# Stick-breaking attention: from running sums by TensorE on transposed scores to VectorE's scan over reversed keys

## The reference, cut to what matters

```python
def stick_breaking_attention(q, k, v):
    ...
        z = jnp.einsum('bqhd,bshd->bhqs', qb, k, preferred_element_type=jnp.float32) * scale
        mask = kpos[None, :] < tpos[:, None]
        log_keep = jnp.where(mask, jax.nn.log_sigmoid(-z), 0.0)
        after = lax.cumsum(log_keep, axis=3, reverse=True) - log_keep
        a = jnp.where(mask, jnp.exp(jax.nn.log_sigmoid(z) + after), 0.0)
        return jnp.einsum('bhqs,bshd->bqhd', a.astype(v.dtype), v)
```

## Time and profile before

| what | value |
|---|---|
| median of 3 runs | 3250.41 us (3246.34 to 3252.65) |
| profiled execution | 3254.31 us, span 3252.7 us |
| PE / PEld / DVE / ACT / POOL busy | 94% / 81% / 69% / 40% / 25% of the span |
| first pair's units of `stick` start on PE | 206.76 us |
| loop of `stick`, first scores to the first matmul of `out_proj` | 225.47 to 365.30 us |

### The profile page before, as it was taken

How to read it: one execution, slowest core, us unless ns; L and a number is a source line. 1 busy time by engine, 2 the same in 40 slices (tenths; PEclk the granted TensorE clock), 3 DMA queues, 4 the chain that set the end, 5 groups by cost and what they waited for, 6 DMA issues and landing times. The chain is left out here.

```text
span 3252.7 us, 43626 instructions
## 1 busy us (share of the span) xinstructions
PE 3064.3 (94%) x16416; PEld 2637.4 (81%) x16416; DVE 2232.9 (69%) x4289; ACT 1292.6 (40%) x2261; POOL 824.2 (25%) x732
## 2 busy tenths in 40 slices
PE   7999899999999999988889988889999999999998
PEld 6666688887666888867768767889999999999998
DVE  4765477674555776753433358988788888888886
ACT  3655432233444322333432232349843443333333
POOL 1001200001001200042000023779734333433431
PEclk9999899999999999989999989999999999999999
DMA  4011144433211544311122222546699999999993
GB/s 145 25 35 46 46 156 136 141 110 119 78 61 63 169 136 141 110 66 54 36 68 91 86 82 75 185 138 229 231 359 325 321 315 316 326 319 328 316 320 117
DMA packets 187616, 522.29 MB, mean 161 GB/s; under 512 B 15616, under 2 KB 78080, under 8 KB 185104
## 3 DMA queue, kind: packets, MB, share of 16 engines
q1 hardware_dynamic: 129344, 307.27, 27.8%
q0 software_dynamic: 45104, 164.68, 14.8%
q10 hardware_dynamic: 12960, 47.55, 3.8%
HBM read 482.71 MB, written 36.73 MB: 160 GB/s over the span
## 5 line engine op out<-in xcount | busy, mean ns | idle before, releaser
L238 PE MATMUL bank<-h_hi,w_hi 128*128 128x512 f32 (+1 forms) x2528 | 964.2, 381 | 61.7 <-DVE h_lo L304 13.0
L238 PE MATMUL bank<-h_lo,w_hi 128*128 128x512 f32 (+1 forms) x2528 | 949.1, 375 | 0.0
L212 DVE TENSOR_TENSOR w_lo<-w_raw,w_hi 128x1024 fp32r<-128x1024 f32 (+1 forms) x460 | 590.2, 1283 | 309.5 <-ACT w_hi L206 307.2
L206 ACT ACTIVATE w_hi<-w_raw 128x1024 fp32r<-128x1024 f32 (+1 forms) x508 | 545.0, 1073 | 522.9 <-PE bank L238 505.0
L238 PE MATMUL bank<-h_hi,w_lo 128*128 128x512 f32 (+1 forms) x2528 | 597.0, 373 | 9.5 <-POOL w_lo L219 9.5
L238 PEld LDWEIGHTS bank<-h_hi,w_hi 128*128 128x128 f32 x2528 | 484.5, 192 | 145.9 <-issue 44.1
L238 PEld LDWEIGHTS bank<-h_lo,w_hi 128*128 128x128 f32 x2528 | 485.3, 192 | 64.7 <-issue 8.7
L238 PEld LDWEIGHTS bank<-h_hi,w_lo 128*128 128x128 f32 x2528 | 460.3, 189 | 79.7 <-issue 13.0
L238 PE MATMUL bank<-e_hi,w_hi 128*128 128x384 f32 x1024 | 345.7, 338 | 8.9 <-DVE e_lo L2357 8.9
L238 PE MATMUL bank<-e_lo,w_hi 128*128 128x384 f32 x1024 | 344.7, 337 | 0.0
L2266 POOL DMA_INDIRECT own_row<-in_u_rows,own_e x128 | 157.6, 1231 | 297.0 <-DVE sums L2394 249.0
(11 more groups left out here) (420 smaller groups left out, 4333.4 us busy)
## 6 DMA issues: line engine op xcount, KB each, us to landing
w_raw<-in_w SPq DMA_DIRECT2D x476, 512.0 KB, 3.8
ada_w<-in_ada_w POOLq DMA_DIRECT2D x48, 512.0 KB, 3.6
expert_weights<-G ACTq DMA_DIRECT2D x12, 2048.0 KB, 7.1
Gin<-expert_weights SPq DMA_DIRECT2D x32, 768.0 KB, 9.7
w_raw<-in_w SPq DMA_DIRECT2D x32, 704.0 KB, 4.1
hidden_ahead<-u_stage ACTq DMA_DIRECT2D x48, 192.0 KB, 2.8
ahead<-hidden_ahead SPq DMA_DIRECT2D x24, 384.0 KB, 6.5
fx_crow<-fox_cum POOLq DMA_DIRECT2D x8, 512.0 KB, 5.5
```

Source lines behind the costliest of these rows:

```text
L206: sc.activation(w_hi[s][:, 0:n], w_raw[raw_slot[u]][:, 0:n], ACT.Copy).then_inc(*w_hi_made.next(u))
L212: ve.tensor_tensor(w_lo[s][:, 0:n], w_raw[raw_slot[u]][:, 0:n], w_hi[s][:, 0:n], ALU.subtract).then_inc(*w_lo_made.next(u))
L238: m = te.matmul(out, wt, moving, start=(not low and k == 0 and moving is hi), stop=(low and k == len(blocks) - 1))
```

## The change

Queries are put on partitions and keys along the free axis, as in `fox`. k and v are written reversed along the sequence (`flip`), so that a running sum from the left is the sum over later keys. Step i of a pair takes the block of queries i by its (i+1)*128 visible keys, the nearest first. DVE scales the scores and adds the mask into `z`, makes `low` = min(-z, 0), and runs one `tensor_tensor_scan` that adds `low` and subtracts `soft` = log(1 + exp(-|z|)) along the keys; adding `z` gives the exponent. ACT makes `soft` in three operations and the exp. PE turns the probabilities block by block, ACT moves them, PE multiplies them with v. The scan, the addition and the exp of a step are issued one step behind its scores, turning, moving and value sums two steps behind. The matmuls of mask and running sums, the high and low parts and GpSimd's share go.

```diff
             split_lo(U[n] + 1)
             yield
             ve.wait_ge(*w_used.at(U[n]))
+            to = dst[:, ::-1] if flip and n else dst[:, :]
-                scaled(dst[:, :], lin[U[n] % 2][:, :]).then_inc(*dve.next(name, "qkv"[n], p))
+                scaled(to, lin[U[n] % 2][:, :]).then_inc(*dve.next(name, "qkv"[n], p))
...
+        neg = sb(st, "sb_neg", [P, T])
+        z = [[sb(st, f"sb_z{hh}{b}", [P, T]) for b in range(2)] for hh in range(2)]
+        neg_in = loaded("sb_neg_in")
+        soft = [[sb(st, f"sb_soft{hh}{b}", [P, T]) for b in range(2)] for hh in range(2)]
+        low = [[sb(st, f"sb_low{hh}{b}", [P, T]) for b in range(2)] for hh in range(2)]
+        Pm = [[sb(st, f"sb_p{hh}{b}", [P, T]) for b in range(2)] for hh in range(2)]
+        PT = [[sb(st, f"sb_pt{hh}{b}", [P, TT, P]) for b in range(2)] for hh in range(2)]
...
-            for m in range(steps + 1):
-                p, n, w, behind, diag = place(m)
-                old = (m - 1) % 2
-                if n == 0:
+            for m in range(steps + 2):
+                p, i = divmod(m, TT)
+                p2, i2 = divmod(m - 2, TT)
...
-                        if m >= 2:
-                            te.wait_ge(*dve.at("sb sum", hh, m - 2))
-                        if n2:
-                            te.matmul(t_bank[hh][:, behind2], rest[:, :], hi[m % 2][:, behind2], start=False, stop=False, skip_group_check=True)
-                            te.matmul(t_bank[hh][:, behind2], rest[:, :], lo[m % 2][:, behind2], start=False, stop=False, skip_group_check=True)
-                for hh in range(2):
...
-                run(more, 4)
+                            te.wait_ge(*dve.at("sb z", hh, m - 1))
+                        te.matmul(s_bank[hh][:, 0:kw], q[p % 2][rows, i * P:(i + 1) * P], k[p % 2][rows, T - kw:T], start=True, stop=True).then_inc(*pe.next("sb scores", hh, m))
                 run(more, 2)
-                if m:
-                    for hh in range(2):
-                        rows = head_rows(hh)
-                        j = TT - 1 - n2
-                        te.wait_ge(*act.at("sb power", hh, m - 1))
-                        if n2 == 0 and p2:
-                            te.wait_ge(*dve.at("sb out", p2 - 1))
-                        t = te.matmul(o_bank[rows, diag2], v[p2 % 2][:, j, rows], ls[hh][old][:, diag2], start=(n2 == 0), stop=False)
-                        if n2:
-                            t = te.matmul(o_bank[rows, behind2], v[p2 % 2][:, j, rows], ls[hh][old][:, behind2], start=False, stop=(j == 0))
-                        t.then_inc(*pe.next("sb sums", hh, m - 1))
-                run(more, 2 if n < TT - 1 else 1 << 30)
+                if m >= 2:
+                    for hh in range(2):
+                        te.wait_ge(*act.at("sb probs", hh, m - 2))
+                        for j in range(i2 + 1):
+                            t = te.transpose(t_bank[hh][:, j * P:(j + 1) * P], Pm[hh][m % 2][:, j * P:(j + 1) * P], ident[:, :])
+                        t.then_inc(*pe.next("sb turned", hh, m - 2))
+                run(more, 2)
+                if m >= 2:
+                    for hh in range(2):
+                        te.wait_ge(*act.at("sb moved", hh, m - 2))
+                    if i2 == 0 and p2 >= 2:
+                        te.wait_ge(*dve.at("sb out", p2 - 2))
+                    for j in range(i2 + 1):
+                        for hh in range(2):
+                            rows = head_rows(hh)
+                            t = te.matmul(o_banks[p2 % 2][rows, i2 * P:(i2 + 1) * P], v[p2 % 2][:, TT - 1 - i2 + j, rows], PT[hh][m % 2][:, j, :],
+                                          start=(j == 0), stop=(j == i2))
+                            if j == i2:
+                                t.then_inc(*pe.next("sb sums", hh, m - 2))
+                run(more, 2 if i < TT - 1 else 1 << 30)
...
+            sc.dma_start(neg[:, 0:P], tabs("before_neg", P)).then_inc(*neg_in.next("in"))
...
+                        t = soft[hh][m % 2][:, 0:kw]
+                        sc.wait_ge(*dve.at("sb z", hh, m))
+                        if m >= 2:
+                            sc.wait_ge(*dve.at("sb left", hh, m - 2))
+                        sc.activation(t, z[hh][m % 2][:, 0:kw], ACT.Abs).then_inc(*act.next("sb abs", hh, m))
+                    for hh in range(2):
+                        t = soft[hh][m % 2][:, 0:kw]
+                        sc.wait_ge(*act.at("sb abs", hh, m))
+                        sc.activation(t, t, ACT.Exp, scale=-1.0).then_inc(*act.next("sb exp", hh, m))
+                if m >= 2:
+                    for hh in range(2):
+                        sc.wait_ge(*pe.at("sb turned", hh, m - 2))
+                        sc.activation(PT[hh][m % 2][:, 0:i2 + 1, :], t_bank[hh][:, 0:(i2 + 1) * P].rearrange("p (j q) -> p j q", q=P),
+                                      ACT.Copy).then_inc(*act.next("sb moved", hh, m - 2))
+                if m < steps:
+                    for hh in range(2):
+                        t = soft[hh][m % 2][:, 0:kw]
+                        sc.wait_ge(*act.at("sb exp", hh, m))
+                        sc.activation(t, t, ACT.Ln, bias=1.0).then_inc(*act.next("sb log", hh, m))
                 run(more, 1)
+                if 1 <= m <= steps:
+                    for hh in range(2):
+                        pm = Pm[hh][(m - 1) % 2][:, 0:kw1]
+                        sc.wait_ge(*dve.at("sb power", hh, m - 1))
+                        sc.activation(pm, pm, ACT.Exp).then_inc(*act.next("sb probs", hh, m - 1))
+                run(more, 1 if i < TT - 1 else 1 << 30)
...
+            run(pair_vector(U[0], buffers, 0, "sb", 0, flip=True))
+            ve.memset(neg[:, P:T], 0.0).then_inc(*dve.next())
+            ve.wait_ge(*neg_in.at("in"))
+            ve.wait_ge(*dve.here())
...
+                    for hh in range(2):
+                        ve.wait_ge(*pe.at("sb scores", hh, m))
                         if m >= 2:
-                            ve.wait_ge(*pe.at("sb sums", hh, m - 2))
-                        ve.tensor_scalar(ls[hh][m % 2][:, w], s_bank[hh][:, w], SCALE, 0.0, ALU.mult, ALU.min).then_inc(*dve.next("sb min", hh, m))
+                            ve.wait_ge(*dve.at("sb power", hh, m - 2))
+                        ve.scalar_tensor_tensor(z[hh][m % 2][:, 0:kw], s_bank[hh][:, 0:kw], SCALE, neg[:, 0:kw], ALU.mult, ALU.add).then_inc(*dve.next("sb z", hh, m))
+                    for hh in range(2):
+                        ve.wait_ge(*dve.at("sb z", hh, m))
+                        if m >= 2:
+                            ve.wait_ge(*dve.at("sb left", hh, m - 2))
+                        ve.tensor_scalar(low[hh][m % 2][:, 0:kw], z[hh][m % 2][:, 0:kw], -1.0, 0.0, ALU.mult, ALU.min).then_inc(*dve.next("sb low", hh, m))
+                if 1 <= m <= steps:
+                    for hh in range(2):
+                        pm = Pm[hh][(m - 1) % 2][:, 0:kw1]
+                        ve.wait_ge(*act.at("sb log", hh, m - 1))
+                        ve.wait_ge(*dve.at("sb low", hh, m - 1))
+                        if m >= 3:
+                            ve.wait_ge(*pe.at("sb turned", hh, m - 3))
+                        ve.tensor_tensor_scan(pm, low[hh][(m - 1) % 2][:, 0:kw1], soft[hh][(m - 1) % 2][:, 0:kw1], 0.0, ALU.add, ALU.subtract).then_inc(*dve.next("sb left", hh, m - 1))
+                    for hh in range(2):
+                        pm = Pm[hh][(m - 1) % 2][:, 0:kw1]
+                        ve.wait_ge(*dve.at("sb left", hh, m - 1))
+                        ve.tensor_tensor(pm, z[hh][(m - 1) % 2][:, 0:kw1], pm, ALU.add).then_inc(*dve.next("sb power", hh, m - 1))
+                run(more, 2 if i < TT - 1 else 1 << 30)
+                if m >= 2 and i2 == TT - 1:
                     ve.wait_ge(*act.at("sb out", p2))
-                    ve.tensor_tensor(o_lo[:, p2, :], o_bank[:, :], o_hi[:, p2, :], ALU.subtract).then_inc(*dve.next("sb out", p2))
-        def gpsimd():
...
-                    gp.wait_ge(*act.at("sb hi", hh, m))
-                    gp.tensor_tensor(lk_lo[hh][m % 2][:, w], lk[hh][:, w], lk_hi[hh][m % 2][:, w], ALU.subtract).then_inc(*pool.next("sb lo", hh, m))
+                    ve.tensor_tensor(o_lo[:, p2, :], o_banks[p2 % 2][:, :], o_hi[:, p2, :], ALU.subtract).then_inc(*dve.next("sb out", p2))
-        gpsimd()
...
-    put("strict_t", (r[:, None] < r[None, :]).astype(np.float32))
-    put("tri", (r[:, None] > r[None, :]).astype(np.float32))
+    put("before_neg", np.where(P - 1 - r[None, :] < r[:, None], 0.0, NEG).astype(np.float32))
```

More of the change, by code:

```diff
@@ L949, in pair_tensor, with pair_vector @@
         yield
-    def pair_vector(U, buffers, s, name, p, gain=None):
+    def pair_vector(U, buffers, s, name, p, gain=None, flip=False):
         q, k, v, vT = buffers
@@ L1006, in tensor @@
                         if m:
-                            te.wait_ge(*dve.at("sb keep", hh, m - 1))
```

(53 more changed lines are left out.)

83 lines of the change are left out of this document (10 added, 73 removed).

## The result

The changed kernel takes 3233.00 us (median of 5 runs, 3226.77 to 3236.77) against 3250.73 us for the kernel before (median of 5, 3246.34 to 3255.19): ratio 0.9944, 95% interval 0.9932 to 0.9956, a gain of 17.7 us. Forecast were 3226, within 3209 to 3240. The profiled execution took 3233.0 us, with a span of 3231.5 and a mean granted clock of 0.971 (before: 3254.3, 3252.7 and 0.971).

What follows compares the result with a forecast made beforehand. PE was the fullest engine before; after, a ring of DVE, ACT and splits would bound pairs. Loop 28.8 us less, clock 5.5 back, net 23.3: 3254.3 to 3231, less 3.9 and one for slack, 3226; range 3209 to 3240.

Steps and rivals of the forecast that it cites:

- PE as the fullest engine before: First pair of the old loop: PE busy 27.6 of 31.1 us, ACT 18.6, DVE 18.4.
- i = 3: Last step of a pair: PE ends it at 8.2 us, including 2.5 from v scaled to first scores.
- `fox` runs at 25.0 us a pair: Stage with the same PE operations a pair, PE busy 24.2 us, clock 1.00; taken as PE's new floor.
- the ring: DVE, ACT and the units' splits wait for each other from z to z: 29.2 us a middle pair.
- a rival at 25.0: PE bounds the loop as in `fox`: pairs two and three cost 25.0 us, total 3217; chance 0.12.
- Durations: New DVE operations: scan 0.43, 0.70, 0.96, 1.22 us by width; low 216 and 479 ns; reversed writes no extra.
- The clock: Lower PE clock takes back 5.5 us: 1 in each middle pair, 1.5 in the emptying, 2 at the output projection.
- half-clock rival: Lower clock holds throughout the loop: 174 us against 139.8, 34 slower, total 3284; chance 0.06.
- The rule quoted for it: Transposes do not count as busy PE as matmuls do, so the loop's clock would fall more often; no size given.
- The stagger does nothing: Rival: each step in the loop still waits for its own turning; given no chance apart.
- the one for unused slack: Last term of the total: rounded down by one us for slack left unused in a pair's last step, giving 3226.
- the forecast's last sign of being wrong: Prediction wrong altogether if stages other than `stick` and the output projection's first window change.

Runs made afterwards that it cites:

- e1: Changed kernel with ACT's split_hi of the next unit issued before the exp of the step behind; 3237.66 us, ratio 0.9957 to the kernel before.
- e2: Changed kernel with the scan replaced by a plain subtraction, running sum left out; 3236.07 us, ratio 0.9951 to the kernel before.
- e5: Changed kernel with split_lo of the units inside the loop moved from DVE to POOL; 3235.85 us, ratio 0.9948 to the kernel before.
- e11: Changed kernel with each score matmul issued twice; 3238.95 us, ratio 0.9957 to the kernel before.
- e7: Changed kernel with PE doing the last two pieces of a pair's last unit before the value sums; 3231.03 us, ratio 0.9939 to the kernel before.
- e3: Changed kernel with idle matmuls into an unread bank on PE in the last pair; 3227.99 us, ratio 0.9927 to the kernel before.
- e8: Changed kernel with e7's order of pieces and e3's idle matmuls together; 3221.19 us, ratio 0.9908 to the kernel before.
- e9: e8 with e1's earlier split_hi added; 3223.89 us, ratio 0.9918 to the kernel before.
- e6: Kernel before without the matmuls of the low part of the running sums, waits kept; 3258.07 us, ratio 1.0023 to the kernel before.
- e4: Changed kernel with scan, addition and exp in their scores' step, turning, moving and value sums one behind; 3265.51 us, ratio 1.0039 to the kernel before.

## Why the prediction was right, step by step

**PE as the fullest engine before: right,** and it was the bound: 30.64 us of work and 3.52 of idle time at the boundary make the 34.16. After the change the same sum is 27.04 + 1.81 = 28.85. So a middle pair gains 3.6 us of PE's work and 1.7 us at the hand-over of v. The prediction gave the first all its attention and the second none: its i = 3 kept the 2.5 us from scaling v to first scores.

**"`fox` runs at 25.0 us a pair": wrong.** The earlier trace rows was a window of 25 us cut by hand, no period. From one pair's second step of scores to the next pair's, `fox` takes 27.5 in the kernel before, with 26.7 us of PE:

```profile
865.10:892.58 27.48, 26.70 (x154) 18.72 (x153) 16.34 (x47) 11.42 (x29) 0.53 (x1) 1.00 0.23 77
```

PE's steps came out short as well: 6.0 and 6.6 us were worked out for the first two, 6.48 and 7.08 measured from scores to scores, and 6.02 and 9.27 for the others. Had the floor been right, 27.0 us of work plus the hand-over would have been seen to be as long as the ring, and PE's bound would have been the forecast and not a rival at 25.0.

**The ring: right in sum, wrong in cause.** Starts of z on DVE in the second pair, and what DVE waits for:

```profile
249.34 0.49 DVE L1085 SCALAR_TENSOR_TENSOR sb_z<-bank,sb_neg 128x128 f32<-128x128 f32 x2 [1.92 <-PE bank L1002]
...
255.17 1.23 DVE L212 TENSOR_TENSOR w_lo<-w_raw,w_hi 128x1024 fp32r<-128x1024 f32 x1 [1.65 <-ACT w_hi L206]
256.31 0.75 DVE L1085 SCALAR_TENSOR_TENSOR sb_z<-bank,sb_neg 128x256 f32<-128x256 f32 x2
...
263.32 1.02 DVE L1085 SCALAR_TENSOR_TENSOR sb_z<-bank,sb_neg 128x384 f32<-128x384 f32 x2 [0.36 <-PE bank L1002]
...
269.61 1.28 DVE L1085 SCALAR_TENSOR_TENSOR sb_z<-bank,sb_neg 128x512 f32<-128x512 f32 x2
...
278.18 0.49 DVE L1085 SCALAR_TENSOR_TENSOR sb_z<-bank,sb_neg 128x128 f32<-128x128 f32 x2 [1.92 <-PE bank L1002]
```

Steps of 6.97, 7.01, 6.29 and 8.57 us stand against the forecast 7.4, 7.0, 6.6 and 8.2: 28.84 against 29.2. The waits are the foretold ones too, DVE's split_lo for ACT's split_hi among them (1.65). Yet e1, e2 and e5 each cut this chain and nothing moved, while e11 and e7 moved the pair by what they did to PE. Two chains of nearly one length ran side by side, and that the forecast of one came within 0.4 us of the other is luck. A wait that the trace shows is no proof that it bounds anything. DVE's load was put too high as well, 22.6 us a pair against 20.35, and the slack that was seen at i = 3 was not there: that step took 8.57.

**Durations: right.** Groups by shape on DVE in the loop after (busy us, mean ns):

```profile
L1098 DVE TENSOR_TENSOR_SCAN sb_p<-sb_low,sb_soft 128x512 f32<-128x512 f32 x8 | 9.3, 1206 | 0.0
L1098 DVE TENSOR_TENSOR_SCAN sb_p<-sb_low,sb_soft 128x128 f32<-128x128 f32 x8 | 2.9, 406 | 0.0
L1090 DVE TENSOR_SCALAR sb_low<-sb_z 128x512 f32<-128x512 f32 x8 | 3.0, 416 | 0.0
L1102 DVE TENSOR_TENSOR sb_p<-sb_z,sb_p 128x512 f32<-128x512 f32 x8 | 5.1, 672 | 0.0
L379 DVE TENSOR_TENSOR sb_k<-bank,norm_y 128x512 f32<-128x512 f32 x3 | 2.0, 683 | 0.0
L379 DVE TENSOR_TENSOR sb_q<-bank,norm_y 128x512 f32<-128x512 f32 x3 | 2.0, 680 | 0.0
```

1206 and 406 ns against 1.22 and 0.43 us; 938 and 673 ns at 384 and 256 columns against 0.96 and 0.70. The scan does pay by the column as worked out from one width, `low` took 416 where 479 was taken, and the reversed write of k costs what the straight one of q does (683 and 680).

**The clock: right in the tail, a matter of chance in the middle.** 1.5 us in the emptying and 2 at the projection were charged; e3 gives back 1.50 and 2.19. The 1 us in each middle pair is 1.6 where it occurs and otherwise nothing. The half-clock rival did not come true: 1.00 in the first pair with its 6 turnings, 1.00 and 0.94 in the next two with 20 each. The rule quoted for it (the Trainium skill, "TensorE: Matmul & The Clock Gate", Part 4 "PE-mode transpose") is not seen at work there, with dense matmuls between; whether the turnings have a share in the last pair's 0.63 was not separated, and the kernel before, without them, had 0.67 and 0.70 in its last pair.

**The stagger: given no weight, and decisive.** "The stagger does nothing" was the one rival left without a chance; rightly, but the same kernel one step behind is 3265.51 us. The prediction worked out the ring for two steps of distance and never what one would have cost, so it did not say how much of the gain hangs on the distance.

**The total: 7 us too low.** The loop was to lose 28.8 and the clock to take 5.5, net 23.3. In the profiled executions the loop got 25.1 shorter and the projection 2.1 longer, 23.0 net: right on that scale. The loop, with 3.5 us for the clock in it, was forecast at 114.5 and measured at 114.7. This closeness is partly luck too: the middle pairs together were put 1.1 us too high (60.4 against 59.30), the last 1.3 too low (29.0 against 30.32; its terms add up to 27.3 and not to the 27.5 that the forecast gives, before the clock's 1.5). The whole execution went from 3254.3 to 3233.0 where 3231 was forecast; the gain of the stage and what other stages added by chance do not separate closer than that. So the term that missed is the last one, the way from this execution to the median, 3.9 us and the one for unused slack. The 3.9 us were taken off as if the excess lay anywhere; but at least as much lay in the very stage that was replaced, whose two slow boundaries were worth 4.7 us of the loop's 6.0 over its repeat. Taken out once from the gain (23 - 6 = 17) the median of 3250.4 gives 3233. That it lands on the measured number to the us is more than one profile on each side can promise. Nor could the forecast's last sign of being wrong, that other stages change, be read from them: the stretch between `oneA` and `e_hi` differed by 6.5 us, but it ranges from 204.2 to 211.4 among versions of the changed kernel that do not touch it.

## What to carry to other kernels

Measure a period from one instruction to the same instruction a period later, never by a window of a round number, and put the full sum of an engine's work in it beside each chain: when the two differ by less than a few per cent, name both as the bound. Read the granted clock beside every stage's length before you take the stage as typical or call an engine not the bound: one episode of lower clock here costs a pair 1.6 us, and the first pairs of e8 and e9 show how easily that passes for the work of an edit. When a stage without dense work stands ahead of one that lives on PE, idle matmuls into a free bank are worth trying (3.7 us here); and look at what stands at a hand-over (v to the first scores) before the arithmetic: one line of order was worth 1.2 us a pair.

## What the runs showed that was not expected

- A kernel with matmuls taken away was slower: e6, 1.0023 (1.0012 to 1.0033), with a lower mean clock in each of its ten runs than in any beside it of before. In its loop the lower clock took back what the edit saved; why the whole program lost 6 us is open.
- Idle matmuls made one faster: e3 issues more and has the ratio 0.9927 (0.9914 to 0.9940), where the changed kernel has 0.9944 and 0.9952 in its two measurements.
- One step of distance less between engines cost 25 us in a loop of 115 (e4), at equal instructions. Of the 8.7 us of a middle pair 6.6 are idle time (8.46 against 1.81), the rest is the lower clock after it.
